# The modulation's sums over partitions as matmuls inside the feed-forwards, and logits of 72 rows, in a three-block fp32 transformer kernel

## What is computed

```python
# block 2: modulation, from c alone, not from x
mod = jax.nn.silu(c) @ ada_w + ada_b            # (1024) @ (1024 x 6144)
sh1, sc1, g1, sh2, sc2, g2 = split(mod, 6)
h = rms_norm(x, mix_pre_g) * (1.0 + sc1) + sh1
# forgetting attention: 8 heads of 64, queries in two blocks of 128
log_f = log_sigmoid(f_logit + b_f); cum = cumsum(log_f)          # per head
s = q . k / sqrt(64) + cum[t] - cum[s]          # then causal mask, softmax, times v
# feed-forward
x = x + ... (silu(h @ W_g) * (h @ W_u)) @ W_out
```

## Time and profile before

| | us |
|---|---|
| median of 3 runs | 1318.49 (1316.56 to 1318.83) |
| the profiled execution | 1319.73, its span 1317.9 |
| TensorE matmuls busy | 1213.8 (92%) |
| VectorE busy | 849.3 (64%) |
| ScalarE busy | 616.0 (47%) |
| chain that ended last: TensorE, VectorE, ScalarE | 72%, 16%, 8% of the span |
| mean granted clock of TensorE | 0.953 |

### The profile page before, as it was taken

The page is one execution under the profiler, slowest core; times in us unless marked ns, Lnnn a source line. Parts: engine busy times, 40 slices in busy tenths (PEclk is TensorE's granted clock), DMA queues, the critical chain, the costliest instruction groups (busy, mean ns, idle before and its releaser), DMA issues.

```text
span 1317.9 us, 21169 instructions
## 1 busy us (share of the span) xinstructions
PE 1213.8 (92%) x9046; PEld 1164.0 (88%) x9046; DVE 849.3 (64%) x1272; ACT 616.0 (47%) x738; POOL 0.2 (0%) x4
## 2 busy tenths in 40 slices
PE   5888978899999999789789999999899998999996
PEld 5678978899999987789789999999797887899996
DVE  6984463777676788844637776767775647644443
ACT  7565315464334355653154643343564347443343
POOL 0000000000000000000000000000000000000000
PEclk9999989999999999999899999999898798999998
DMA  9454322565868663544325658786443203455510
GB/s 346 124 174 128 128 96 65 170 214 173 273 228 278 212 207 91 179 128 128 96 65 179 205 178 270 240 273 214 154 146 110 96 1 128 160 189 171 184 65 33
DMA packets 177614, 214.15 MB, mean 162 GB/s; under 512 B 3696, under 2 KB 160752, under 8 KB 177520
## 3 DMA queue, kind: packets, MB, share of 16 engines
q1 hardware_dynamic: 176800, 211.86, 48.7%
q10 hardware_dynamic: 720, 0.94, 0.2%
HBM read 211.74 MB, written 1.05 MB: 161 GB/s over the span
## 4 chain that ended last, share of the span: by engine, by line
PE 72%; DVE 16%; ACT 8%; issue 3%; DMA 1%; SPq 0%; DVEq 0%; ACTq 0%
PE stream L492 16%; PE stream L493 15%; PE stream L494 15%; DVE w_lo L1304 6%; PE steps L494 4%; PE steps L493 4%; PE steps L492 4%; ACT w_hi L881 4%; PE steps L799 2%; PE steps L657 1%; PE stream L676 1%; ACT probs L881 1%; PE stream L580 1%; DMA raw<-in_w_in 1%; PE steps L647 1%
## 5 line engine op out<-in xcount | busy, mean ns | idle before, releaser
L1304 DVE TENSOR_TENSOR w_lo<-raw,w_hi 128x2048 fp32r<-128x2048 f32 (+2 forms) x178 | 402.4, 2266 | 328.2 <-ACT w_hi L881 326.5
L881 ACT ACTIVATE w_hi<-raw 128x2048 fp32r<-128x2048 f32 (+2 forms) x178 | 336.6, 1894 | 415.1 <-PE stream L494 372.0
L492 PE MATMUL stream<-h_hi,w_hi 128*128 128x256 f32 x1576 | 454.4, 288 | 11.7 <-DVE w_lo L1304 6.0
L493 PE MATMUL stream<-h_lo,w_hi 128*128 128x256 f32 x1576 | 449.9, 285 | 0.0
L494 PE MATMUL stream<-h_hi,w_lo 128*128 128x256 f32 x1576 | 449.6, 285 | 0.0
L492 PEld LDWEIGHTS stream<-h_hi,w_hi 128*128 128x128 f32 x1576 | 307.0, 195 | 15.5 <-DVE w_lo L1304 7.8
L493 PEld LDWEIGHTS stream<-h_lo,w_hi 128*128 128x128 f32 x1576 | 306.9, 195 | 0.5 <-issue 0.5
L494 PEld LDWEIGHTS stream<-h_hi,w_lo 128*128 128x128 f32 x1576 | 306.5, 195 | 0.0
L492 PE MATMUL steps<-gu_hi,w_hi 128*128 128x256 f32 x528 | 149.5, 283 | 0.7 <-DVE gu_lo L1561 0.7
L493 PE MATMUL steps<-gu_lo,w_hi 128*128 128x256 f32 x528 | 149.4, 283 | 0.0
L494 PE MATMUL steps<-gu_hi,w_lo 128*128 128x256 f32 x528 | 149.4, 283 | 0.0
(11 more groups left out here) (286 smaller groups left out, 1706.7 us busy)
## 6 DMA issues: line engine op xcount, KB each, us to landing
raw<-in_w_ffn_in SPq DMA_DIRECT2D x66, 1024.0 KB, 5.2
raw<-in_w_in SPq DMA_DIRECT2D x54, 1024.0 KB, 6.0
raw<-in_w_ffn_out SPq DMA_DIRECT2D x33, 1024.0 KB, 6.7
ada_raw<-in_ada_w SPq DMA_DIRECT2D x24, 1024.0 KB, 5.3
raw<-in_w_out SPq DMA_DIRECT2D x8, 1024.0 KB, 5.0
raw<-in_w_proj_attn SPq DMA_DIRECT2D x8, 512.0 KB, 3.5
raw<-in_w_proj_hgrn SPq DMA_DIRECT2D x8, 512.0 KB, 4.6
raw<-in_w_o SPq DMA_DIRECT2D x4, 1024.0 KB, 4.9
```

What stands on the lines that cost most here:

```text
L492: pe.matmul(dst, w_h, x_h, start=start, stop=False, skip_group_check=True)
L493: pe.matmul(dst, w_h, x_l, start=False, stop=False, skip_group_check=True)
L881: return act.activation(out_, in_, func, **kw)
L1304: tt(wl[m % SPL][:, 0:n], raw[m % RAW][:, 0:n], wh[m % SPL][:, 0:n].bitcast(F32), ALU.subtract)\
```

## The change

The sums over partitions move into the feed-forwards of blocks 0 and 1. In step i from 2 on, TensorE, behind gate i, takes the group of blocks that were summed in step i-1: for each block one fp32 matmul with the 128x128 ones stationary and the 256 sums moving, into bank 3 of `S`, which gate and up units of these feed-forwards no longer use. Every row of the result is then the same sum, so VectorE, behind `gu_lo` of step i, takes for each 128 columns the product with the identity and its row sum (`tensor_tensor_reduce`), which leaves channel p's sum in partition p, and adds ada_b. Three steps (5, 7, 8) now have two blocks, where steps 5 and 9 had, and step 10 has none. The gains are made in step 10. Both calls of `modulation` in mixer 1 and block 2 go.

In block 2 q and k are held with one head per slot in 64 partitions, and 8 more rows below them: a one-hot row pattern under q, -8 cum under k. One matmul of 72 rows gives a head's logits. ScalarE copies each unit in two halves and fills the 8 rows, twice 8x2048.

```diff
-ADA_STEP = (1, 2, 3, 4, 5, 5, 6, 7, 8, 9, 9, 10)
+ADA_STEP = (1, 2, 3, 4, 5, 5, 6, 7, 7, 8, 8, 9)
+ADA_GROUPS = [[j for j in range(ADA_LAYER) if ADA_STEP[j] == i] for i in sorted(set(ADA_STEP))]
 ADA_AFTER = {UFF[b] + n: ADA_LAYER * b + j for b in range(2)
-             for j, n in enumerate((3, 6, 11, 14, 17, 20, 23, 24, 26, 29, 32, 35))}
+             for j, n in enumerate((3, 6, 11, 14, 17, 20, 23, 25, 27, 30, 31, 34))}
...
# plan_banks: bank 3 is left out for gate and up of blocks 0 and 1
+                if bank == 3 and u[0] in ("gate", "up") and u[1] < 2:
+                    bank = 0
...
# TensorE
-        def modulation(b):
-            for e, c in BANKS[ada_unit[b]][1]:
-                pe.wait_ge(evac[e], c)
-            pe.wait_ge(ada_summed, ADA_LAYER * (b + 1))
-            for j in range(2 * ADA_LAYER):
-                mm = pe.matmul(S[ada_bank[b]][:, j:j + 1], ada_sum[:, j // 2, P * (j % 2):P * (j % 2) + P], ones[:, 0:1],
-                               start=True, stop=True)
-            mm.then_inc(ada_done, 1)
+        def modulation(b, g):
+            if g == 0:
+                pe.wait_ge(evac[MOD_FREE[b][0]], MOD_FREE[b][1])
+            if b or g:
+                pe.wait_ge(ada_read.sem, len(ADA_GROUPS) * b + g)
+            for n, j in enumerate(ADA_GROUPS[g]):
+                pe.wait_ge(ada_summed, ADA_LAYER * b + j + 1)
+                pe.matmul(S[3][:, UC * n:UC * n + UC], ones, ada_sum[:, j, :], start=True, stop=True).then_inc(ada_done, 1)
...
# TensorE, attend: logits
-                mm = pe.matmul(dst, qT[o:o + DH, h // 2, qs], kT[o:o + DH, h // 2, 0:n_s], start=True, stop=b < 2)
                 if b == 2:
-                    mm = pe.matmul(dst, ident[o:o + 8, o + h:o + h + 1].broadcast_to([8, P]), cumn[o:o + 8, 0:n_s],
-                                   start=False, stop=True)
+                    mm = pe.matmul(dst, qa[0:DH + H, h, qs], ka[0:DH + H, h, 0:n_s], start=True, stop=True)
+                else:
+                    mm = pe.matmul(dst, qT[o:o + DH, h // 2, qs], kT[o:o + DH, h // 2, 0:n_s], start=True, stop=True)
...
# TensorE, feed_forward
-            stream(3 * FS - 5, normed(2 * b + 1))
+            before = normed(2 * b + 1)
+            for i in range(2, FS):
+                stream(1, before)
+                before = None
+                if i - 1 in ADA_STEP:
+                    modulation(b, sorted(set(ADA_STEP)).index(i - 1))
+                stream(2)
+            stream(1)
...
# ScalarE, block 2
-        for i, dst in enumerate((qT, kT)):
+        act.wait_ge(ada_done, 2 * ADA_LAYER)
+        f(qa[DH:DH + H], ident[DH:DH + H, DH:DH + H].unsqueeze(2).broadcast_to([H, H, T]), ACT.Copy).then_inc(*lane.step())
+        for i, dst in enumerate((qa, ka)):
             for j in range(2):
                 tick()
                 unit_in()
-                f(dst[:, 2 * j:2 * j + 2, :], b2(here()), ACT.Copy).then_inc(*emptied())
+                for n in range(2):
+                    ins = f(dst[0:DH, 4 * j + n:4 * j + 4:2, :], b2(here())[DH * n:DH * n + DH], ACT.Copy)
+                    ins.then_inc(*(emptied() if n else lane.step()))
...
                 diagonals(2 * i + j)
+                if (i, j) == (0, 1):
+                    act.wait_ge(*c_cum.at(0))
+                    f(ka[DH:DH + H], lfa.unsqueeze(1).broadcast_to([H, H, T]), ACT.Copy, scale=-1.0 / SCALE)\
+                        .then_inc(*lane.mark(c_rows))
...
# VectorE
+        def modulation(b, g):
+            for n, j in enumerate(ADA_GROUPS[g]):
+                dve.wait_ge(ada_done, ADA_LAYER * b + j + 1)
+                for c in range(2):
+                    col = 2 * (ADA_LAYER * b + j) + c
+                    dve.tensor_tensor_reduce(mod_term[:, 2 * n + c], S[3][:, UC * n + P * c:UC * n + P * c + P], ident, 1.0, 0.0, ALU.mult,
+                                             ALU.add, flat_mod[:, col:col + 1]).then_inc(*lane.step())
+            dve.wait_ge(*lane.last)
+            n = 2 * len(ADA_GROUPS[g])
+            cols = flat_mod[:, 2 * (ADA_LAYER * b + ADA_GROUPS[g][0]):][:, 0:n]
+            tt(cols, cols, pc("ada_b", 2 * (ADA_LAYER * b + ADA_GROUPS[g][0]), n), ALU.add).then_inc(*lane.mark(ada_read))
...
# VectorE, feed_forward, behind gu_lo and ahead of sum_ada
+                if b < 2 and i - 1 in ADA_STEP:
+                    modulation(b, sorted(set(ADA_STEP)).index(i - 1))
+                    if i - 1 == ADA_STEP[-1]:
+                        gains(b)
                 for j in range(ADA_LAYER if b < 2 else 0):
                     if ADA_STEP[j] == i:
                         sum_ada(ADA_LAYER * b + j)
```

More of the change, by code:

```diff
@@ L152, in plan_banks @@
 def plan_banks():
-    count, bank, last, out = {"act": 0, "dve": 0, "gu": 0}, 0, {}, []
+    count, bank, last, out, free_at = {"act": 0, "dve": 0, "gu": 0}, 0, {}, [], []
     for u in UNITS:
+        if u[0] == "gate" and u[1] < 2 and u[2] == 0:
+            free_at.append(last[3])
+            last[3] = ("mod", len(ADA_GROUPS) * (u[1] + 1))
         e = evac_engine(u)
@@ L172, in plan_banks @@
         out.append((banks, free, count[e] if e else 0))
-    return out
-BANKS = plan_banks()
+    return out, free_at
+BANKS, MOD_FREE = plan_banks()
 def build(nc, a, out):
@@ L206, in build @@
     kT = at("kT", [P, 4, T], F32, 140)
+    qa = at("q_and_pick", [P, H, T], F32, 128)
+    ka = at("k_and_cum", [P, H, T], F32, 136)
     yh_h = at("yh_hi", [P, 4, T], F32R, 136)
@@ L245, in build @@
     cv = at("conv_acc", [P, 4, T], F32, 188)
-    diag = [at(f"conv_diagonal{j}", [P, P], F32, (194, 155, 148, 132)[j // 8] + 0.5 * (j % 8)) for j in range(CONV_K)]
+    diag = [at(f"conv_diagonal{j}", [P, P], F32, (194, 155, 148, 124)[j // 8] + 0.5 * (j % 8)) for j in range(CONV_K)]
     yc_h = at("conv_out_hi", [P, 4, T], F32R, 148)
@@ L280, in build @@
     gain = small("gain2", [P, 4, KC])
+    flat_mod = mod.rearrange("p j c -> p (j c)")
+    mod_term = at("modulation_term", [P, 4, P], F32, 142)
     rs_t = small("rstd_of_token", [P, NT])
@@ L353, in build @@
     x2_new = Event("x2_updated", 4)
-    ada_out = Event("ada_evacuated")
-    ada_unit = (U0[1] + 4, U0[2] + 2)
-    ada_bank = [BANKS[m][0][0] for m in ada_unit]
+    ada_read = Event("modulation_read", len(ADA_GROUPS))
+    evac["mod"] = ada_read.sem
     gains_set = Event("gains_set")
@@ L381, in build @@
     c_diag, c_tap, c_pe = Event("diagonals_set", 4), Event("last_chunk_summed"), Event("last_chunk_set")
+    c_rows = Event("cum_rows_set")
     c_f, c_cum, c_conv, c_ms, c_mu, c_cen, c_sq, c_var, c_rs, c_aff, c_act, c_hi, c_lo = (
@@ L731, in mixer @@
             stream(1)
-            if b == 1:
-                modulation(0)
             pe.wait_ge(*i_rot.at(b, 0))
@@ L832, in _ @@
         norm_sum(4)
-        modulation(1)
         stream(1)
         stream(5, normed(4))
-        pe.wait_ge(*c_cum.at(0))
+        pe.wait_ge(*c_rows.at(0))
         first = attend(2, 0, [evacuated(unit(2, "k1"))])
@@ L1247, in _ @@
                 unit_in()
-                f(dst[:, 2 * j:2 * j + 2, :], b2(here()), ACT.Copy).then_inc(*emptied())
+                for n in range(2):
+                    ins = f(dst[0:DH, 4 * j + n:4 * j + 4:2, :], b2(here())[DH * n:DH * n + DH], ACT.Copy)
+                    ins.then_inc(*(emptied() if n else lane.step()))
+                if i and j:
+                    act.wait_ge(*n_lo.upto(4))
                 diagonals(2 * i + j)
+                if (i, j) == (0, 1):
+                    act.wait_ge(*c_cum.at(0))
+                    f(ka[DH:DH + H], lfa.unsqueeze(1).broadcast_to([H, H, T]), ACT.Copy, scale=-1.0 / SCALE)\
+                        .then_inc(*lane.mark(c_rows))
         first, second = attend(2, 0), attend(2, 1)
@@ L1388, in normalise, with gains @@
             low(3)
[L1390 to L1395, removed]
+        def modulation(b, g):
[9 more added lines that the diff above has]
+            tt(cols, cols, pc("ada_b", 2 * (ADA_LAYER * b + ADA_GROUPS[g][0]), n), ALU.add).then_inc(*lane.mark(ada_read))
+        def gains(b):
+            dve.wait_ge(*lane.last)
+            if b == 0:
+                ts_(gain[:, 0, :], mod[:, 1, :], 1.0, None, ALU.add).then_inc(*lane.step())
+                dve.wait_ge(*lane.last)
+                tt(gain[:, 0, :], gain[:, 0, :], pc("mix_pre", 0, 8), ALU.mult).then_inc(*lane.mark(gains_set))
+                return
+            ts_(gain[:, 1, :], mod[:, 4, :], 1.0, None, ALU.add).then_inc(*lane.step())
+            tt(gain[:, 2, :], mod[:, 2, :], pc("mix_post", 0, 8), ALU.mult).then_inc(*lane.step())
+            tt(gain[:, 3, :], mod[:, 5, :], pc("ffn_post", 0, 8), ALU.mult).then_inc(*lane.step())
+            dve.wait_ge(*lane.last)
+            tt(gain[:, 1, :], gain[:, 1, :], pc("ffn_pre", 0, 8), ALU.mult).then_inc(*lane.mark(gains_set))
         def rotate(x, n, cos, sin):
@@ L1520, in feed_forward @@
             if b == 1:
-                dve.wait_ge(ada_done, 1)
+                dve.wait_ge(ada_done, ADA_LAYER)
```

(4 more changed lines are left out.)

3 lines of the change are left out of this document (removed).

## The result

The changed kernel takes 1331.9 us (median of 4 runs, 1330.3 to 1334.4) beside 1318.5 for the kernel before (4 runs, 1316.6 to 1318.8): ratio 1.0106, 95% interval 1.0088 to 1.0125. It is 1.1% slower. A second set of runs gave 1.0098 (1.0077 to 1.0118). The forecast was 1321.5, with a range up to 1329: the direction was right, the size was not.

What follows compares the result with a forecast made beforehand. TensorE, busy 92% of the span, was taken as the bound. +10.3 + 18.8 + 7.5 - 4.3 - 6.5 - 22.8 = +3.0 us on the 1318.5 median gave 1321.5 us; own range 1317 to 1326, whole 1310 to 1329.

Steps and rivals of the forecast that it cites:

- Part 1: Feed-forwards, TensorE's own work: 24 fp32 matmuls of 256 columns at 0.43 us each, +10.3 us.
- Part 2: Feed-forwards: TensorE waits for VectorE's sums in steps 5, 7 and 8, none in single-sum steps; +18.8 us.
- the sign of being wrong: Feed-forwards: TensorE waiting in single-sum steps, VectorE fuller than counted, would refute the forecast; no size given.
- Part 3: Feed-forwards: half clock behind five of six new waits, 1.5 us each, +7.5 us.
- Part 4: Ends of the feed-forwards: a sum goes from step 10, the second's end wait and low stretch go; -4.3 us.
- part 5: Mixer 1: without the modulation matmuls VectorE normalises without its gap and qk_sumsq starts sooner; -6.5 us.
- Part 6: Block 2: modulation gone, 72-row logits without switching, less half clock, ScalarE late with k1; -22.8 us.
- (a): Feed-forwards and block 2: over half the price of low stretches doesn't come, 1315 us; chance 0.20.
- (b): Block 2: ScalarE's chain 3 us shorter through cheaper fills, gains and losses cancel, 1318.5 us; chance 0.20.
- (c): Block 2: ScalarE's chain longer, from 7 us on TensorE's wait for k1 is 12 us, 1328 us; chance 0.20.
- (d): Feed-forwards: VectorE sums before TensorE arrives, so the waits are hidden, 1295 us; chance 0.05.

Runs made afterwards that it cites:

- the first two runs: The changed kernel with each group of sum matmuls one unit later (1298.9 us), and with each group 12 matmuls later (1314.7 us).

## Why the prediction was wrong, point by point

**Part 1, the 24 matmuls: right.** 10.2 us against 10.3.

**Part 2, the waits: mechanism right, count wrong.** The six waits forecast came as 2.87, 3.13, 3.15 and 2.87, 2.87, 3.15: 18.0 us against 18.8. The step that failed is "in a step with one sum ... no wait": I read VectorE's queue in step 5 and took it for all. Step 1 is another: 2.2 us in each feed-forward, +4.4, which the prediction had named as the sign of being wrong. It could be read before. In the trace of the kernel before, the sum of step 1 ends at 314.72 + 3.61 = 318.33, and TensorE begins up 2 at 316.14:

```profile
314.72 3.61 DVE L1514 SCALAR_TENSOR_TENSOR ada_sum<-ada_raw,c_act,ada_sum 128x256 f32<-128x256 f32 x7
...
316.14 0.28 PE L492 MATMUL stream<-h_hi,w_hi 128*128 128x256 f32 x1
```

That is 2.2 us, the wait that came. In all +3.6 us.

**Part 3, the clock: price right, count too low, and the restart at nothing.** I had five low stretches at 1.5 us. The price holds, by the two traces of feed-forward 1, but the trace has seven (eight in the second). And each wait costs some 0.25 us of restart at full clock, a term that I had nowhere. Feed-forwards: 46.05 = 10.2 (matmuls) + 22.4 (waits) + 7 x 1.5 = 10.5 (low stretches) + 2.9. The 2.9 is what is left over, restarts above all, eight in number; the low clock lengthens the matmuls of the sums too. (The expectations of the first two runs price a low stretch at 1.7, half its length; but a streamed matmul takes 0.12 us at full clock and 0.21 at half, so it loses less than half.) For the last two terms I had 7.5: +5.9 us, the largest single error. I had let one row at 2.69 us without a fall weigh against waits that were all longer; behind those of 2.86 us and more the clock fell every time.

**Part 4 and part 5: right.** From the end of feed-forward 0 to `h_norm` of mixer 1 the time fell by 1.6 us (1.5). VectorE in mixer 1, which answers to the earlier trace rows and the second row:

```profile
514.67 1.67 DVE L1403 SCALAR_TENSOR_TENSOR h_norm<-xT,params,rstd 128x256 f32<-128x256 f32 x4
...
519.04 1.48 DVE L1398 TENSOR_TENSOR h_lo<-h_norm,h_hi 128x512 fp32r<-128x512 f32 x2
520.44 4.49 DVE L1323 TENSOR_TENSOR w_lo<-raw,w_hi 128x2048 fp32r<-128x2048 f32 x2
524.84 1.21 DVE L1451 TENSOR_REDUCE qk_sumsq<-qk_square 128x16 f32<-128x1024 f32 x1
```

Normalising is 5.8 us without the gap (5.76), and qk_sumsq starts 10.2 us behind `h_norm` where it was 17.1. With the 1.6 that is 8.5; the forecast had 8.0. The measured 12.1 holds 3.6 more, in the attention and the recurrence behind. It goes with less half clock there; in the five traces with the groups one unit later mixer 1 is 8.3 to 8.8 us shorter than before, in the second trace of the changed kernel 10.6. Whether the 3.6 are chance or come with the changed kernel stays open, as both its traces lie on the same side. So the account by parts holds for 8.5, and the rest made the forecast look better than it was.

**Part 6, block 2: right.** 23.7 us came of the 25.6 with the end of feed-forward 1. The wait for k1 is 5.4 (5), the one for conv_in 4.1 (4), the way to the logits 9.5 us shorter (10), and from there to the conv matmuls it is 14.2 shorter (15.6). ScalarE's chain from the table load to k1 started 11.9 us sooner, as forecast, and took 25.9 us (25.4) instead of 23.5. The cost of the fills and half copies was wrong only in the expectation for the run with the old logits, which has 5.5 us: without them the way to the logits is 11.9 us shorter than before, so they cost 2.4. The rows tell why. With the old logits ScalarE stands idle before each of its last four splits, 0.81 to 1.02 us and 3.8 in all, waiting for TensorE; the last of them:

```profile
976.62 1.91 ACT L889 ACTIVATE w_hi<-raw 128x2048 fp32r<-128x2048 f32 x1 [1.01 <-PE stream L501]
```

In the changed kernel the same split follows without idle time:

```profile
1015.24 1.90 ACT L890 ACTIVATE w_hi<-raw 128x2048 fp32r<-128x2048 f32 x1
```

The added work of ScalarE, 2 x 1.9 us of fills and 4 x 0.6 of copies, first fills these 3.8 us, and only what is over counts.

**The rivals.** (a), that over half of the low stretches stay away, and (b), a shorter ScalarE chain, did not come. (c) named ScalarE's chain as the cost; a longer kernel came, but not through it. (d), the waits hidden, had the right price (1295 against 1298.9 and 1296.05 measured) but needs another place for the group than the change gave it.

**The sum of errors**: waits +3.6, clock and restart +5.9, matmuls -0.1, mixer 1 -4.1, block 2 +1.9, the clock of mixer 0 +1.6: with the rounding +8.9 us over the 3.0, 11.9 measured. The feed-forwards alone were 9.4 us worse than forecast; the 4.1 of mixer 1 hid part of that. The range ended at 1329 because it was drawn around ScalarE's chain. The waits had bounds of 15 and 22 with six stretches at most, and never the case of a seventh and eighth.

## What to carry to other kernels

Work put into the solid queue of the bounding engine costs its own time and no more if its operand is ready when the engine gets there. So compare the two queues' positions step by step, the odd first and last steps of the loop too, and move the insertion by a unit until the last of them has slack: here one line's move turned +1.1% into -1.5%. Price a wait of TensorE of about 3 us in full-clock work at its length plus 1.7 to 1.9 us, as measured here on the units behind waits of 2.86 to 3.15. And when an engine late at a point also waits for the engine that you wish to feed, cutting its work returns only the part up to that wait, and work added to it first fills the time in which it stood idle.

## What the runs showed of the hardware

Behind 12 of 12 waits on ada_sum of 2.86 to 3.15 us, in otherwise full-clock work, the granted clock fell to half (1.2 GHz) for 3.4 us, which cost 1.5. Behind those of 2.1 to 2.6 us it fell in 5 of 10, a wait of 2.42 with and one of 2.57 without in the same trace; behind 10 waits of 0.7 to 1.9 it never fell. The same wait of 2.2 us in step 1 of feed-forward 1 was followed by it in one trace and not in the other.

A matmul of fp32 with 256 columns and the ones stationary, dropped singly or in pairs into the stream, costs 0.42 us, and two of a single column with 128x128 of sums stationary cost 0.44. One of a single column thus takes 0.22, about half of one with 256: its price doesn't go by its moving columns.

The same mixer code took from 277.7 to 283.5 us with 23.9 to 37.5 us at half clock. A difference of 3 us between single traces of that stretch says nothing of an edit.
